# Twelve landing buffers for the expert weights, a combination of five tiles on TensorE, and separate banks for the last down product

## The chip, the cores and the metric

The kernel runs on one core of a Trainium2 chip. The metric is the device time of one execution in microseconds (us), the median of several runs. The core has TensorE (PE in the profile, its weight loads PEld), VectorE (DVE), ScalarE (ACT), GpSimd (POOL) and SyncE (SP, which issues nearly all plain DMAs), and 16 DMA engines.

## What is computed

One layer of a hybrid encoder for 1024 tokens of width 1024, in float32: a combined projection, latent attention, a spatial gating unit, an output projection, and then the part that matters here, a top-2 mixture of 32 experts, and a final RMSNorm:

```python
x = x + _hier_moe(_rmsnorm(x, g_ffn_norm[l]), ...)     # 32 experts, each token in two of them
    hid = jax.nn.silu(xb @ w_eg[e]) * (xb @ w_eu[e])   # 1024 x 256 each, for a block of 128 rows
    ys  = hid @ w_ed[e]                                # 256 x 1024
    out = zeros.at[buf_tok].add(ys * buf_w[:, None])   # the two results of a token, weighted
return _rmsnorm(x, g_final)
```

## The kernel before

The kernel is written engine by engine, in one instruction stream for each, with semaphores between them. Its stages follow one another: projection, attention, gating, output projection ("W", with the router, "R", in between), the experts ("E") and the combination ("C"). Products are made in a split float32: each operand is a high part (rounded to what TensorE multiplies in one pass) and a low part (the rest), and `mm3` (L374 to L378) issues three matmuls, high by high, low by high, high by low.

**Expert stage.** There are 36 blocks of up to 128 token rows: blocks 0 to 31 are the first of each expert, the others the overflow. `experts(eng, body)` runs the blocks on each engine in groups of four: a group written out, a loop over the middle groups, and a last group written out. A block needs three weight pieces of 1 MB (gate, up, down), so there are 108 pieces, numbered n by `piece`. A piece takes this way:

1. SP loads it into one of six landing buffers, `raw_e[n % 6]` (L499). The load waits until DVE has made the low part of piece n - 6 (`w_lo_ready`).
2. ACT writes its high part into `we_hi[n % 4]` (`high`, L1166), once TensorE has used piece n - 4 (`group_used`).
3. DVE writes its low part, landing buffer minus high part, into `we_lo[n % 4]` (`low`, L1646).
4. TensorE uses both (`columns` for gate and up, `down` for down; L376 to L378).

The token rows of a block come by an indirect DMA (a gather, L1773) from `h2_dram` into one of four buffers `xs`, three or four blocks ahead. TensorE transposes them (`rows_in`, L898), ACT and DVE split them (`rows_high` L1170, `rows_low` L1650). A block's result is copied by ACT from PSUM banks 5 and 6 to `y` (`rows_out`, L1184), and POOL sends it to `y_dram` by an indirect DMA (`scatter`, L1793), after copying a column of row numbers (`ycol`, L1789). On TensorE block j is: gate of j + 1, transposes of the hidden values of j (L918), up of j + 1, down of j, `rows_in` of j + 3. For the last two blocks the same code runs with the parts left out that have no following block.

**Combination.** For each of eight tiles of 128 tokens, SP loads the token's two expert results, `yin[t][:, 0]` and `yin[t][:, 1]` (L540), 512 KB each, behind the final gain `g_fin` (L534), once all results have been sent. DVE computes gate0 * yin0 + x2 (L1696), adds gate1 * yin1 (L1697), ACT sums the squares (L1219) and takes the root (L1221), DVE scales by it and by `g_fin` (L1706), SP stores. The fifth to eighth tile's loads wait for the first tiles' sums (`acc_ready`).

**Order around the change.** Each engine runs its stream as written; what moves work is only the order of the code and the semaphores. SP loads the first three pieces while the output projection runs, three more when its last tile is under way, and the rest in stage E.

## Time and profile before

| | us |
|---|---|
| median of 3 runs | 1217.96 (1217.54 to 1220.79) |
| the profiled execution | 1214.95 |
| its span, first to last instruction | 1213.1 |
| PE busy | 1108.3 (91% of the span) |
| DVE busy | 733.7 (60%) |
| ACT busy | 563.4 (46%) |
| POOL busy | 344.2 (28%) |

Times in the text count from the start of the span. The stages after the attention: the output projection and the router to 798, the experts from there to 1168, the combination to the end. In the experts' part PE is busy all the time and so is the DMA; in the last 43 us PE does nothing. The chain of waits (the work that ended last, followed back) is 72% PE, 12% DVE, 6% DMA and 5% ACT.

### The profile page before, as it was taken

What the parts mean: (1) busy time and instruction counts of PE and PEld (TensorE: products, weight loads), DVE (VectorE), ACT (ScalarE), POOL (GpSimd) and SP (SyncE); (2) the same over time, 40 slices, a digit from 0 to 9 for tenths busy, and PEclk for the clock granted to TensorE, in tenths of its full rate; (3) what the DMA queues carried; (4) which work ended last, traced back from release to release, by engine and by line L of the source; (5) the groups of instructions that cost most, each with busy time, mean ns of one, the idle gap of its engine ahead of it and who ended that gap; (6) DMA issues with size and microseconds to landing.
All of it is one profiled execution on the core that took longest, in us unless ns stands there. A gap on an engine that the chain in (4) does not pass through costs nothing.

```text
span 1213.1 us, 18702 instructions
## 1 busy us (share of the span) xinstructions
PE 1108.3 (91%) x6931; PEld 964.6 (80%) x6931; DVE 733.7 (60%) x948; ACT 563.4 (46%) x759; POOL 344.2 (28%) x273
## 2 busy tenths in 40 slices
PE   5998999999999999999999899979999999999930
PEld 4876888888877878888888688778999999989930
DVE  7875666666045632222112655579888888888938
ACT  6235555655135200000002322248888888778823
POOL 1403322112332222233320000034444444555310
PEclk9998999999999989999999999989999999999975
DMA  8010000020203111121102433448999999999747
GB/s 242 10 29 11 7 7 7 6 71 19 69 1 97 35 35 52 52 52 38 49 18 101 131 113 130 157 170 321 393 389 361 366 352 371 350 366 365 292 156 286
DMA packets 94174, 184.31 MB, mean 152 GB/s; under 512 B 30752, under 2 KB 68128, under 8 KB 80288
## 3 DMA queue, kind: packets, MB, share of 16 engines
q1 hardware_dynamic: 83744, 166.65, 39.2%
q0 software_dynamic: 10368, 16.80, 3.7%
q8 instruction: 42, 0.69, 0.2%
q14 instruction: 20, 0.16, 0.0%
HBM read 177.12 MB, written 27.26 MB: 168 GB/s over the span
## 4 chain that ended last, share of the span: by engine, by line
PE 72%; DVE 12%; DMA 6%; ACT 5%; issue 3%; SPq 1%; POOL 0%; ACTq 0%; DVEq 0%; POOLq 0%
PE ps L376 22%; PE ps L378 21%; PE ps L377 21%; DMA raw_e<-in_w_exp_gate_dram 4%; DVE we_lo L1646 2%; PE ps L898 2%; PE ps L666 2%; DVE pt_lo L1389 1%; PE ps L827 1%; DVE negm L1344 1%; ACT we_hi L1166 1%; DVE q_tmp L1335 1%; ACT prob L1039 1%; DVE acc L1696 1%; DVE res L1706 1%
## 5 line engine op out<-in xcount | busy, mean ns | idle before, releaser
L1646 DVE TENSOR_TENSOR we_lo<-raw_e,we_hi 128x2048 fp32r<-128x2048 f32 x108 | 246.9, 2287 | 40.2 <-ACT we_hi L1166 38.5
L1166 ACT ACTIVATE we_hi<-raw_e 128x2048 fp32r<-128x2048 f32 x108 | 206.2, 1911 | 17.7 <-DMA raw_e<-in_w_exp_gate_dram 6.7
L376 PE MATMUL ps<-ht_hi,w_hi 128*128 128x512 f32 x448 | 176.0, 393 | 0.5 <-DVE ht_lo L1262 0.4
L378 PE MATMUL ps<-ht_hi,w_lo 128*128 128x512 f32 x448 | 174.5, 389 | 0.0
L377 PE MATMUL ps<-ht_lo,w_hi 128*128 128x512 f32 x448 | 174.4, 389 | 0.0
L376 PE MATMUL ps<-we_hi,xst_hi 128*128 128x256 f32 x576 | 168.7, 293 | 0.0
L378 PE MATMUL ps<-we_hi,xst_lo 128*128 128x256 f32 x576 | 162.8, 283 | 0.0
L377 PE MATMUL ps<-we_lo,xst_hi 128*128 128x256 f32 x576 | 162.7, 283 | 0.0
L370 POOL CAST w_hi<-raw 128x1024 fp32r<-128x1024 f32 x36 | 39.5, 1097 | 297.1 <-PE ps L378 250.6
L1468 DVE TENSOR_TENSOR mix<-ps,mix 128x512 f32<-128x512 f32 x16 | 11.1, 691 | 168.1 <-PE ps L378 168.1
L376 PEld LDWEIGHTS ps<-we_hi,xst_hi 128*128 128x128 f32 x576 | 110.5, 192 | 0.2 <-issue 0.2
L377 PEld LDWEIGHTS ps<-we_lo,xst_hi 128*128 128x128 f32 x576 | 110.3, 191 | 0.0
L378 PEld LDWEIGHTS ps<-we_hi,xst_lo 128*128 128x128 f32 x576 | 110.1, 191 | 0.0
L376 PEld LDWEIGHTS ps<-ht_hi,w_hi 128*128 128x128 f32 x448 | 84.1, 188 | 18.3 <-POOL w_lo L371 0.8
L378 PEld LDWEIGHTS ps<-ht_hi,w_lo 128*128 128x128 f32 x448 | 84.1, 188 | 17.7
L377 PEld LDWEIGHTS ps<-ht_lo,w_hi 128*128 128x128 f32 x448 | 84.2, 188 | 17.2 <-issue 0.2
L371 POOL TENSOR_TENSOR w_lo<-raw,w_hi 128x1024 fp32r<-128x1024 f32 x36 | 88.3, 2454 | 2.9
L1105 ACT ACTIVATE mix<-ps 128x512 f32<-128x512 f32 x16 | 8.7, 597 | 147.0 <-PE ps L378 147.0
L1789 POOL COPY ycol<-yidx 128x1 uint32 (+1 forms) x36 | 27.4, 762 | 149.3 <-ACT y L1184 149.3
L1389 DVE TENSOR_TENSOR pt_lo<-ps,pt_hi 128x512 fp32r<-128x512 f32 (+2 forms) x96 | 50.5, 553 | 20.9 <-ACT pt_hi L1065 20.6
L376 PE MATMUL ps<-we_hi,hidt_hi 128*128 128x512 f32 x144 | 57.2, 397 | 4.8 <-DVE hidt_lo L1660 4.7
L1065 ACT ACTIVATE pt_hi<-ps 128x512 fp32r<-128x512 f32 (+2 forms) x96 | 43.5, 488 | 36.8 <-PE ps L666 36.8
(295 smaller groups left out, 2561.9 us busy)
## 6 DMA issues: line engine op xcount, KB each, us to landing
raw_e<-in_w_exp_gate_dram SPq DMA_DIRECT2D x36, 1024.0 KB
raw_e<-in_w_exp_up_dram SPq DMA_DIRECT2D x36, 1024.0 KB
raw_e<-in_w_exp_down_dram SPq DMA_DIRECT2D x36, 1024.0 KB
raw<-in_w_in_dram SPq DMA_DIRECT2D x27, 512.0 KB, 3.9
yin<-y_dram SPq DMA_DIRECT2D x16, 512.0 KB, 6.6
xin<-in_x_dram SPq DMA_DIRECT2D x8, 512.0 KB, 7.8
raw<-in_w_out_dram SPq DMA_DIRECT2D x8, 512.0 KB, 3.8
xre<-in_x_dram SPq DMA_DIRECT2D x8, 512.0 KB, 5.7
```

Of the source, the lines that this page charges most:

```text
L370: pool_link(pool, pool.tensor_copy(w_hi[n % 3][:, :, :], raw[n % 3][:, :, :]))
L371: pool.tensor_tensor(w_lo[n % 3][:, :, :], raw[n % 3][:, :, :], w_hi[n % 3][:, :, :].bitcast(F32), ALU.subtract).then_inc(sem("w_split"), 1)
L376: pe.matmul(dst, st[0], mv[0], start=first, stop=False)
L377: pe.matmul(dst, st[0], mv[1], start=False, stop=False)
L378: return pe.matmul(dst, st[1], mv[0], start=False, stop=last)
L666: mm = pe.transpose(ps[:, bank_of(0, c0 + c), (j % 4) * P:(j % 4) * P + P], prob[s % 2][:, j * P:(j + 1) * P], ident[:, :])
L898: mm = pe.transpose(ps[:, k // 4, (k % 4) * P:(k % 4) * P + P], v[:, k, :], ident[:, :])
L1065: act.activation(pt_hi[cc % 4][:, 0:w, :].rearrange("p a b -> p (a b)"), ps[:, bank_of(0, cc), 0:w * P], ACT.Copy).then_inc(sem("pt_hi_rea ...
L1166: act.activation(we_hi[c % 4][:, :], raw_e[c % 6][:, :], ACT.Copy).then_inc(sem("w_hi_ready"), 1)
L1389: dve.tensor_tensor(pt_lo[cc % 4][:, 0:w, :].rearrange("p a b -> p (a b)"), ps[:, bank_of(0, cc), 0:w * P], pt_hi[cc % 4][:, 0:w, :].rearr ...
L1646: dve.tensor_tensor(we_lo[c % 4][:, :], raw_e[c % 6][:, :], we_hi[c % 4][:, :].bitcast(F32), ALU.subtract).then_inc(sem("w_lo_ready"), 1)
L1789: pool.tensor_copy(ycol[j % 2][:, :], yidx[:, c]).then_inc(sem("ycol_ready"), 1)
```

## The change

1. **Landing buffers.** There are twelve `raw_e` (NS = 12) in place of six. `we_lo` has no buffers of its own: it lies on the landing buffer of the same piece, so DVE's subtraction writes over what it reads. The load of piece n waits for `group_used` of piece n - 12. `xs` has two buffers instead of four; the gather of block j + 4 waits for the transposes of block j + 2 instead of block j. SP issues two pieces more during the last tiles of stage W (one of them ahead of the last `xre` load, one ahead of the last store of `h2`) and four more at the start of stage E. The loop runs from 0 and adds 1 to its number.
2. **Last blocks.** On ACT and DVE the last down piece's high and low part come before SiLU and the hidden product of the last block, and ACT copies the last but one result after the last block's hidden values. The last down product goes to banks 0 and 1, and TensorE does 8 idle transposes (`keep_on`) ahead of it. POOL copies `ycol` before it waits for the result.
3. **Combination.** `g_fin` is loaded at the end of stage E. All `yin` loads are issued at once; tile 0's two halves have a semaphore each. For tiles 2, 3, 5, 6 and 7 TensorE computes gate0 * yin0 + gate1 * yin1 as four float32 matmuls with diagonal matrices `diag` (two DVE operations make them), and DVE adds `x2` from PSUM. ACT loads the table of the square root beforehand. TensorE does 64 idle transposes before these products.

```diff
+        NS = 12
+        slots = (8, 16, 24, 172, 180, 188, 196, 92, 100, 116, 124, 164)
+        raw_e = [at(f"raw_e{i}", slots[i], [P, 2048], F32) for i in range(NS)]
+        we_lo = [at(f"we_lo{i}", slots[i], [P, 2048], F32R) for i in range(NS)]
+        ON_PE = (2, 3, 5, 6, 7)
...
             for j in range(4):
                 body(0, j, lambda n: True)
             eng.wait_ge(sem("blocks_ready"), 1)
-            with eng.Fori(1, end) as it:
+            with eng.Fori(0, end) as it:
                 for j in range(4):
-                    body(it, j, lambda n: True)
+                    body(it + 1, j, lambda n: True)
...
-                    wait(sp, "w_lo_ready", n - 5)
+                    wait(sp, "group_used", n - (NS - 1))
...
                         load(0, 0, 2)
+                        load(1, 0, 2)
+                sp.wait_ge(sem("out_done"), NT + 1)
+                sp.wait_ge(sem("x2_ready"), NT + 1)
+                load(2, 0, 1)
                 sp.wait_ge(sem("h2_ready"), NT)
                 sp.dma_start(h2_dram[(NT - 1) * P:NT * P, :], ...)
...
+                sp.wait_ge(sem("group_used"), end * 12 + 1)
+                sp.dma_start(g_fin[:, :], ...)
                 for i in range(2):
                     sp.wait_ge(sem(f"y_sent{i}"), end * 32 + 32)
             if "C" in on:
-                sp.dma_start(g_fin[:, :], ...)
                 for t in range(NT):
-                    if t >= 4:
-                        sp.wait_ge(sem("acc_ready"), t - 3)
...
@@ TensorE
-                    pe.wait_ge(sem(f"xs_full{j % 4}"), (it + (j // 4 + 1)) * 16)
+                    pe.wait_ge(sem(f"xs_full{j % 2}"), (it * 2 + (j // 2 + 1)) * 16)
...
-                    wait(pe, "y_ready", it * 4 + j)
+                    wait(pe, "y_ready", it * 4 + j - last)
...
-                            mm = mm3(pe, ps[:, 5 + half, :], ...)
+                            mm = mm3(pe, ps[:, (0 if last else 5) + half, :], ...)
...
+            if "C" in on:
+                keep_on(64, 7)
+                pe.wait_ge(sem("z_diag_ready"), 3)
+                for n, t in enumerate(ON_PE):
+                    pe.wait_ge(sem(f"rows_full{t}"), 48)
+                    if n >= 2:
+                        pe.wait_ge(sem("acc_ready"), ON_PE[n - 2] + 1)
+                    for c in range(2):
+                        for k in range(2):
+                            mm = pe.matmul(ps[:, 2 * (n % 2) + c, :], diag[k][:, t, :], yin[t][:, k, c * HALF:(c + 1) * HALF],
+                                           start=k == 0, stop=k == 1)
+                    mm.then_inc(sem("spread_done"), 1)
...
@@ DVE
+                    if t in ON_PE:
+                        n = ON_PE.index(t)
+                        dve.wait_ge(sem("spread_done"), 3 + n)
+                        dve.tensor_tensor(acc[t % 2][:, :], ps[:, 2 * (n % 2):2 * (n % 2) + 2, :]..., x2[:, t, :],
+                                          ALU.add).then_inc(sem("acc_ready"), 1)
+                        return
...
@@ POOL
-                    pool.wait_ge(sem("y_ready"), it * 4 + (j + 1))
                     wait(pool, f"y_sent{j % 2}", it * 32 + 8 * (j - j % 2))
                     pool.tensor_copy(ycol[j % 2][:, :], yidx[:, c]).then_inc(sem("ycol_ready"), 1)
...
+                    pool.wait_ge(sem("y_ready"), ready)
                     pool.indirect_dma_start(y_dram, ...)
...
-                        pool.wait_ge(sem("xs_tr"), it * 4 + (j + 1))
+                        pool.wait_ge(sem("xs_tr"), it * 4 + (j + 3))
```

SP's queue from the last tiles of stage W into stage E, before (`xre` is the residual's input, `h_dram<-h` the store of a normalised tile):

```order
L508 DMA h_dram<-h_174 128x1024 [waits h2_ready]
L499 DMA raw_e_225<-in_w_exp_up_dram 128x2048 [waits mt_lo_ready]
L499 DMA raw_e_226<-in_w_exp_down_dram 128x2048
L499 DMA raw_e_227<-in_w_exp_gate_dram 128x2048
L505 DMA xre_171<-in_x_dram 128x1024 [waits x2_ready]
L508 DMA h_dram<-h_173 128x1024 [waits h2_ready]
L520 DMA h_dram<-h_174 128x1024 [waits h2_ready]
L499 DMA raw_e_222<-in_w_exp_up_dram 128x2048 [waits w_lo_ready]
L499 DMA raw_e_223<-in_w_exp_down_dram 128x2048 [waits w_lo_ready]
```

And now:

```order
L510 DMA raw_e_227<-in_w_exp_gate_dram 128x2048
L510 DMA raw_e_228<-in_w_exp_up_dram 128x2048
L516 DMA xre_171<-in_x_dram 128x1024 [waits x2_ready]
L519 DMA h_dram<-h_173 128x1024 [waits h2_ready]
L510 DMA raw_e_229<-in_w_exp_down_dram 128x2048 [waits x2_ready,out_done]
L535 DMA h_dram<-h_174 128x1024 [waits h2_ready]
L510 DMA raw_e_230<-in_w_exp_gate_dram 128x2048
L510 DMA raw_e_231<-in_w_exp_up_dram 128x2048
L510 DMA raw_e_232<-in_w_exp_down_dram 128x2048
L510 DMA raw_e_233<-in_w_exp_gate_dram 128x2048 [waits h2_stored1,h2_stored0]
L510 DMA raw_e_222<-in_w_exp_up_dram 128x2048 [waits group_used]
```

The seventh piece has moved ahead of the last `xre` load, the eighth ahead of the last store of `h2`; the ninth to twelfth follow with no wait for another engine's splitting, and from the thirteenth on a load waits for TensorE.

ACT's queue at the last two blocks, before (L1179 hidden values' high part, L1175 SiLU, L1166 a weight's high part, L1184 copy of a result):

```order
L1179 ACTIVATE hidt_hi<-ps 128x256 [waits hid_tr]
L1173 REGISTER_ALU
L1175 ACTIVATE sg<-ps 128x256 [waits hid_ready,group_used]
L1166 ACTIVATE we_hi_231<-raw_e_227 128x2048 [waits group_used,raw_e_full5]
L1182 REGISTER_ALU
L393 REGISTER_ALU [waits group_used]
L1184 ACTIVATE y_248<-ps 128x1024 [waits y_sent0]
L1179 ACTIVATE hidt_hi<-ps 128x256 [waits hid_tr]
```

And now:

```order
L1213 ACTIVATE hidt_hi<-ps 128x256 [waits hid_tr]
L1200 ACTIVATE we_hi_249<-raw_e_233 128x2048 [waits group_used,raw_e_full11]
L1207 REGISTER_ALU
L1209 ACTIVATE sg<-ps 128x256 [waits hid_ready,group_used]
L1213 ACTIVATE hidt_hi<-ps 128x256 [waits hid_tr]
L1216 REGISTER_ALU
L404 REGISTER_ALU [waits group_used]
L1219 ACTIVATE y_260<-ps 128x1024 [waits y_sent0]
```

The last weight's high part stands ahead of SiLU, and the last hidden values ahead of the copy of the last but one result.

DVE's queue for the last two tiles of the combination, before:

```order
L1696 SCALAR_TENSOR_TENSOR acc_260<-yin_257,gatew,x_172 128x1024 [waits ssq_ready,res_ready,yin_full3]
L1697 SCALAR_TENSOR_TENSOR acc_260<-yin_257,gatew,acc_260 128x1024 [waits dve_step]
L1705 RECIPROCAL rstd<-std 128x1 [waits std_ready]
L1706 SCALAR_TENSOR_TENSOR res_267<-acc_259,rstd,g_fin 128x1024 [waits dve_step]
L1705 RECIPROCAL rstd<-std 128x1 [waits std_ready]
L1706 SCALAR_TENSOR_TENSOR res_268<-acc_260,rstd,g_fin 128x1024 [waits dve_step]
```

And now:

```order
L1747 TENSOR_TENSOR acc_274<-ps,x_172 128x1024 [waits spread_done,ssq_ready,res_ready]
L1762 RECIPROCAL rstd<-std 128x1 [waits std_ready]
L1763 SCALAR_TENSOR_TENSOR res_281<-acc_273,rstd,g_fin 128x1024 [waits dve_step]
L1762 RECIPROCAL rstd<-std 128x1 [waits std_ready]
L1763 SCALAR_TENSOR_TENSOR res_282<-acc_274,rstd,g_fin 128x1024 [waits dve_step]
```

One addition from PSUM, which waits for TensorE, stands in the place of two operations on the loaded rows; so it is for the five tiles named.

## Rows read from the trace of the kernel before

**Rows 1.** Busy time of each engine in stretches of the span, in us.

```profile
core 0: us, PE busy (x) PEld busy (x) DVE busy (x) ACT busy (x) POOL busy (x), PEclk, DMA share, GB/s
775.00:798.00 23.00, 15.35 (x91) 12.54 (x90) 13.44 (x50) 8.71 (x11) 0.00 (x0) 0.90 0.12 47
...
839.00:1022.00 183.00, 183.00 (x1332) 173.57 (x1332) 162.83 (x117) 154.26 (x133) 82.72 (x76) 1.00 0.99 374
1022.00:1094.00 72.00, 69.64 (x501) 65.23 (x501) 60.38 (x43) 57.59 (x50) 34.92 (x28) 1.00 0.97 359
...
1170.00:1213.00 43.00, 0.00 (x0) 0.00 (x0) 31.50 (x32) 12.72 (x25) 0.00 (x0) 0.50 0.80 305
```

**Rows 2.** The same view for L898 alone: PE, PEld, clock, DMA share, GB/s.

```profile
839.20:1142.90 303.70, 33.25 (x256) 33.01 (x256) 1.00 0.98 372
```

**Rows 3.** Chain of waits: start, us, what; L898 x8 transposes one block's rows.

```profile
839.45 0.88 PE ps L898 x8
...
868.31 0.88 PE ps L898 x8
...
1027.67 16.02 DMA raw_e<-in_w_exp_gate_dram
...
1141.94 0.88 PE ps L898 x8
```

**Rows 4.** Timeline of ACT: start, us, line, what, idle before and its releaser.

```profile
1033.35 1.92 ACT L1166 ACTIVATE we_hi<-raw_e 128x2048 fp32r<-128x2048 f32 x1 [0.43 <-DMA raw_e<-in_w_exp_gate_dram]
```

**Rows 5.** Timeline of DVE, SP and POOL at the start of the experts.

```profile
782.34 0.69 DVE L1505 TENSOR_TENSOR x<-ps,xre 128x512 f32<-128x512 f32 x1
...
792.07 0.33 SPq L520 DMA_DIRECT2D h_dram<-h  x1
...
799.45 2.55 POOL L1773 DMA_INDIRECT xs<-h_dram,xidx  x1 [33.57 <-DVE xidx L1594]
```

**Rows 6.** The last `xre` load, issued at 765.2: issue to landing.

```profile
DMA to landing us min/median/max: 10.6/10.6/10.6
```

**Rows 7.** Timeline of POOL: a gather within the expert stage.

```profile
855.06 1.04 POOL L1773 DMA_INDIRECT xs<-h_dram,xcol  x1 [0.76 <-POOL xcol L1778]
```

**Rows 8.** Timeline of ACT and of PE at the last block.

```profile
1157.86 1.91 ACT L1166 ACTIVATE we_hi<-raw_e 128x2048 fp32r<-128x2048 f32 x1
1161.34 0.38 ACT L1179 ACTIVATE hidt_hi<-ps 128x256 fp32r<-128x256 f32 x1
...
1162.67 0.47 PE L376 MATMUL ps<-we_hi,hidt_hi 128*128 128x512 f32 x1 [2.14 <-DVE hidt_lo L1660]
```

**Rows 9.** Timeline of POOL, last scatter; then the chain's next DMA.

```profile
1167.81 0.98 POOL L1793 DMA_INDIRECT y_dram<-y,ycol  x1 [0.76 <-POOL ycol L1789]
...
1170.83 6.05 DMA yin<-y_dram
```

**Rows 10.** The load of `g_fin`, issued at 1170.0: issue to landing.

```profile
DMA to landing us min/median/max: 4.3/4.3/4.3
```

**Rows 11.** DMA in the combination; columns as in group 1.

```profile
1180.00:1185.00 5.00, 0.00 (x0) 0.00 (x0) 4.53 (x5) 3.68 (x7) 0.00 (x0) 0.50 1.03 413
```

**Rows 12.** Last step of the chain; DVE's last operation; additions from PSUM in W.

```profile
1207.06 1.16 ACT junk L1219 x2
...
1208.77 1.28 DVE L1706 SCALAR_TENSOR_TENSOR res<-acc,rstd,g_fin 128x1024 f32<-128x1024 f32 x1
...
L1505 DVE TENSOR_TENSOR x<-ps,xre x9: 691/1225/1225, 686.3 to 788.3; 128x1024 f32<-128x1024 f32 x7, 128x512 f32<-128x512 f32 x2
```

**Rows 13.** Timeline of PE: two float32 matmuls (four records) at full clock.

```profile
63.35 1.88 PE L590 MATMUL ps<-z_diag,ones 128*128 128x512 f32 x4
```

**Rows 14.** PE after a pause; then the clock, as in group 1.

```profile
426.99 0.77 PE L376 MATMUL ps<-ot_hi,w_hi 128*128 128x512 f32 x1 [4.24 <-issue]
...
428.00:431.00 3.00, 3.00 (x9) 2.33 (x8) 0.69 (x1) 0.27 (x1) 0.00 (x0) 0.50 0.00 0
432.00:435.00 3.00, 3.00 (x15) 2.47 (x14) 0.10 (x1) 0.00 (x0) 0.00 (x0) 1.00 0.00 0
```

More of the change, by code:

```diff
@@ L522, in expert @@
                 def expert(it, j, left):
-                    if left(2):
+                    fetched = isinstance(it, int) and it == 0 and j == 0
+                    if left(2) and not fetched:
                         load(1, it, j + 2)
-                    if left(1):
+                    if left(1) and not fetched:
                         load(2, it, j + 1, not left(2))
+                    if isinstance(it, int) and it == 0 and j == 1:
+                        for i in range(2):
+                            sp.wait_ge(sem(f"h2_stored{i}"), 16 * NT // 2)
                     if left(3):
@@ L1183, in rows_out @@
                     wait(act, f"y_sent{j % 2}", it * 32 + 8 * (j - j % 2))
-                    act.activation(y[j % 2][:, :], ps[:, 5:7, :].rearrange("p b c -> p (b c)"), ACT.Copy).then_inc(sem("y_ready"), 1)
+                    b = 0 if last else 5
+                    act.activation(y[j % 2][:, :], ps[:, b:b + 2, :].rearrange("p b c -> p (b c)"), ACT.Copy).then_inc(sem("y_ready"), 1)
                 def expert(it, j, left):
@@ L1189, in expert @@
                         high(1, it, j + 2)
-                    if left(1):
+                    if left(2):
                         silu(it, j + 1)
-                        high(2, it, j + 1, not left(2))
+                        high(2, it, j + 1)
+                    elif left(1):
+                        high(2, it, j + 1, True)
+                        silu(it, j + 1)
+                        return
+                    else:
+                        rows_out(it, j - 1, False)
                     rows_out(it, j, not left(1))
```

95 lines of the change are left out of this document (57 added, 38 removed).

## Prediction

> **What bounds the kernel now.** I first read the busy time by stretch, to see which engine sets the pace where. From 839 to 1022 us TensorE is busy in every one of the 183 us, at full clock, and the DMA share is 0.99; from 1022 to 1094 TensorE is idle for 2.4 us of 72 and the DMA share is still 0.97 [rows 1]. So two things run side by side: TensorE, and a DMA that has hardly a free moment. Then the chain of waits shows the rhythm. The transposes of a block's rows begin at 839.45, and those three blocks on at 868.31: one block in 9.62 us [rows 3]. Up to 1142 there are 256 of them, 32 blocks of 8, so 31 intervals [rows 2]; they end with the block at 1141.94 [rows 3]. At 9.62 us they would take 298.2 us; they took 1141.94 - 839.45 = 302.5. The stage loses 4.3 us against its own rhythm. Where: after 1022 the chain goes through a weight load that took 16.02 us from issue to landing [rows 3], and from 1033 on ACT waits for a landing before each split [rows 4]; before that, in the 183 us at 100% TensorE, nothing was lost. So the landing buffers run empty late in the stage, and the rest of the stage is TensorE's own. Last, the stretch from 1170 on: 43 us with TensorE at zero, DVE busy 31.5 us and the DMA at 0.80 [rows 1]. There DVE is the bound, after some 7 us of waiting for the first load.
>
> The sums are made against the profiled execution: span 1213.1, time 1214.95. The median of the runs, 1217.96, is 3.0 us above it, and I take the difference over to the median unchanged. About 0.3% (3.7 us) is what a measurement of this kernel can tell from no change.
>
> **Twelve landing buffers.** A load of piece n could run ahead of ACT's split by five pieces (six buffers, freed by DVE); now by eight (twelve buffers, freed by TensorE, and ACT's split waits for piece n - 4). Three pieces are one block, 9.62 us more of slack. The shortfall to cover is 4.3 us. The lead has to be built while the DMA is free, for in the stage it is not: between 775 and 798 its share is 0.12 [rows 1], and a 1 MB piece takes 2.5 us at the 413 GB/s of [rows 11]. The two pieces moved into stage W and the four issued at its end are 15 us of transfer, which fit mostly ahead of 806. So I take the whole 4.3 us as gained: **-4.3 us** (bounds: 0, if the DMA is short throughout the stage, and -4.3, since the rhythm of 9.62 us is TensorE's). The first loads in the loop wait for TensorE instead of DVE; SP has nothing else queued behind them in this stage. DVE's subtraction in place has the same size, so the same price.
>
> What the moved loads are in the way of: the last `xre` load was issued at 765.2 and landed 10.6 us later [rows 6], behind three pieces; a fourth makes it 778.3, and DVE reads it at 782.34 [rows 5]: 4 us of cover. The last store of `h2`, issued at 792.07, gets a piece ahead of it, 2.5 us at most; POOL did not wait for it but for DVE's row numbers, until 799.45 [rows 5]: hidden, by about 2 us. The first gather, at 799.45, shares the DMA with the end of pieces nine to twelve, where it shared it with pieces seven and eight before; I take **0**, between -1 us (the warming transposes of TensorE end about then) and +2.5 us (one piece in its way). The loop's other bounds leave TensorE's register instructions in number as they were.
>
> `xs` with two buffers: a gather now waits for the transposes of block j + 2. These run just ahead of the moment at which POOL comes to the gather anyway (in the block before 868.31's but one, transposes at 849.07 = 868.31 - 2 x 9.62, the gather at 855.06 [rows 3, 7]), so it costs 0.
>
> **The last block.** Today ACT splits the last down weight at 1157.86, behind SiLU, copies the last but one result, and comes to the last hidden values at 1161.34; TensorE starts the last down product at 1162.67, after 2.14 us idle [rows 8]. In the new order the hidden values' high part follows their transposes, which end when TensorE goes idle at 1160.5, without the copy between, and the weight is split before: ACT starts it at 1160.5 or a little after instead of 1161.34, and TensorE about 0.9 us earlier. The eight idle transposes (an eighth of a rows' transposing each, 0.88 / 8 us [rows 3]) take 0.9 us, within that pause. **-0.9 us** (0 to -1.2). For the last scatter the column of row numbers is copied beforehand, and the 0.76 us of waiting for it [rows 9] leaves the path: **-0.8 us**.
>
> **Start of the combination.** When the last scatter has landed, SP issues `g_fin` (1170.0) and the first tile, and DVE starts when a load issued at 1170.83 has landed 6.05 us later, at 1176.9 [rows 9]. `g_fin` alone took 4.3 us [rows 10]: that is the time of 512 KB on an empty queue. In the new order the first half of tile 0 stands first on an empty queue, and DVE's first operation needs it alone. With 1.7 us gained above, SP issues it at 1168.3, it lands at 1172.6, and DVE starts 4.3 us earlier than now: **-2.6 us** beyond the 1.7.
>
> **The combination.** For five tiles two DVE operations of 1.28 us give way to one addition from PSUM, which took 1.23 us in stage W [rows 12]; DVE alone would save 5 x 1.3 = 6.6 us. But TensorE and the loads may now be later, so I write out the schedule, on the old time scale (without the 4.3 us). A tile is 1.05 MB, 2.55 us at 413 GB/s [rows 11]; tiles are complete at 1173.9, 1176.4, 1179.0, 1181.5, 1184.1, 1186.6, 1189.1, 1191.7. A float32 matmul of 512 columns is two records; four records took 1.88 us with the last one's tail, 0.43 each from start to start [rows 13]. A tile has four matmuls, eight records: 3.4 us at full clock, 6.8 at half. The 64 idle transposes keep TensorE at work to about 1172, then it waits for tile 2 until 1179.0; after a pause of 4.24 us it stood at 1.2 GHz, and came back to 2.4 GHz within 5 us of work [rows 14]. I take 3.5 us at half clock: tile 2 takes 5.2 us, to 1184.2; then 3.4 each: tile 3 to 1187.6, tile 5 to 1191.0, tile 6 to 1194.4. Tile 7 needs the PSUM banks of tile 5, so DVE's sum of it.
> DVE: tile 0 to 1175.3, tile 1 (from 1176.5) to 1179.1, scaling of 0 to 1180.5. It waits for TensorE, adds tile 2 at 1184.2, scales 1, to 1186.9; tile 3 and scaling 2 from 1187.6 to 1190.3; tile 4 (its own, two operations) and scaling 3 some 4.1 us, to 1194.4; then a pair of 1.23 and 1.28 and the reciprocal, 2.8 us: 5 and 4 to 1197.2, 6 and 5 to 1200.0. Tile 7 on TensorE from 1195.7 to 1199.1: ready. It is summed at 1201.3; the square and the root take 1.7 us (from 1207.06, when the sum was there, to 1208.77 [rows 12]), and the last scaling ends at 1204.3. Before, it ended at 1208.77 + 1.28 = 1210.05 [rows 12]. Of these 5.8 us, 4.3 are the earlier start; the combination itself gives **-1.5 us** (-3 with TensorE at full clock throughout). The two operations that make `diag` (1.2 us each, by the same kind of addition) lie under the last down product and the last scatter, where DVE is idle. The final stores: 4.2 MB, 10 us of transfer from 1191.7 on, done before DVE's last one.
>
> **Sum:** -4.3 - 0.9 - 0.8 - 2.6 - 1.5 = -10.1 us. The profiled execution would take 1204.9, the median 1217.96 - 10.1 = 1207.9.
>
> **Rivals.** *The DMA is short throughout, so the larger buffers only move the wait* (or are never ahead, since loads wait for TensorE): then 4.3 us come back, 1212.2. For it speaks the share of 0.99 even before 1022; against it that the shortfall of 4.3 us is smaller than the four pieces, 10 us, that now land before the stage needs them.
> *TensorE stays at 1.2 GHz in the combination.* Five tiles in a row of 6.8 us from 1179.0 end at 1213.0; plus the addition, 1.7 and the scaling, 1217.2 instead of 1210.05: with the gain of the experts 1217.96 + 7.2 - 4.3 = 1220.9. Against it: [rows 14], where steady work brought the clock back in under 5 us.
> *Gathers come too late* (slower). Place: `rows_in`, on TensorE. The gather at 855.06 is for the transposes at 868.31 [rows 3, 7], 13.2 us later. If a deeper queue of weights holds a gather up, each microsecond beyond 13.2 is lost in each of some 28 blocks. If it had to let eight pieces of 3.2 us pass, 25.7 us, the stage would take 28 x 12.5 = 350 us more; at 14 us of latency 22 us more, about 1234. Decisive is whether the gather waits behind the weights. A weight piece took 16.02 us at 1027 [rows 3] and TensorE never stood still for rows in that stretch, so gathers were faster than the weights queued ahead of them: it is unlikely. The Trainium skill ("DMA: Bandwidth & Descriptors", Queues, rings and completion order) says that an engine takes turns between the rows of queues that have work; by that rule a longer queue of weights doesn't delay a gather, and the trace agrees, as the 16.02 us beside the 13.2 show.
> *Better:* TensorE at full clock from tile 2 on, and the first gather a little earlier: 1204 to 1205.
>
> **Chances.** The forecast (1205 to 1210.5) 0.68; better 0.08; the DMA short, or the start of the experts delayed by a piece (1210.5 to 1213) 0.14; TensorE at half clock (1220.9, within 0.3% or just above) 0.05; gathers late 0.05. So faster by over 0.3% (below 1214.3) 0.90, within 0.3% 0.05, slower 0.05. Range 1203.5 to 1212.5: it leaves out the last two and the edge of the third.
>
> **What would show it.** Right: 31 intervals of 9.62 us for L898's successor, without a DMA in the chain and without ACT waiting for weights after 1000; the last down product 1.2 us after TensorE's last transposes of hidden values instead of 2.1; DVE's first combining operation 4.4 us after the first tile's issue; DVE waiting for TensorE before tiles 2 and 3 by some 4 and 1 us, and not after. Wrong: ACT still waiting for landings late in the stage (first rival); PEclk at 0.5 to the end (second); PE idle before the rows' transposes, released by the gather (third).

## The result, and the profile after

The changed kernel takes **1206.24 us** (median of 4 runs, 1205.61 to 1207.88); the kernel before, over all its runs by then, 1217.75. The ratio is 0.9908, with a 95% interval of 0.9891 to 0.9926. The forecast was 1207.9, the range 1203.5 to 1212.5. The profiled execution took 1206.01, its span is 1204.1, so the two profiled executions lie 8.9 us apart and the medians 11.5.

The busy time by stretch, columns as in [rows 1], which these lines answer to; then the same for L917 alone (L898 before, [rows 2]):

```profile
core 0: us, PE busy (x) PEld busy (x) DVE busy (x) ACT busy (x) POOL busy (x), PEclk, DMA share, GB/s
775.00:798.00 23.00, 15.35 (x93) 12.53 (x91) 13.47 (x50) 8.71 (x11) 0.00 (x0) 0.90 0.48 178
839.00:1022.00 183.00, 183.00 (x1333) 173.58 (x1332) 162.86 (x115) 154.14 (x134) 117.71 (x76) 1.00 0.98 370
1022.00:1094.00 72.00, 72.00 (x526) 68.29 (x525) 63.07 (x46) 60.92 (x53) 45.93 (x31) 1.00 0.99 379
...
1172.00:1179.00 7.00, 3.10 (x4) 1.51 (x5) 3.92 (x4) 2.82 (x6) 0.00 (x0) 0.52 1.02 416
1179.00:1200.00 21.00, 16.16 (x37) 6.57 (x35) 17.28 (x21) 8.66 (x18) 0.00 (x0) 0.99 0.80 317
```

```profile
840.30:1139.80 299.50, 33.25 (x256) 33.14 (x256) 1.00 0.96 365
```

TensorE now works through all of 1022 to 1094, where it stood idle for 2.4 us, and the DMA moves 379 GB/s there in place of 359. Ahead of the stage, from 775 to 798, the DMA share is 0.48 in place of 0.12. In the last stretch TensorE is at work, but from 1172 to 1179 at 1.2 GHz.

The chain of waits (start, us, what), beside [rows 3]:

```profile
799.61 8.68 DMA xs<-h_dram,xidx
808.33 1.17 PE ps L917 x8
...
840.69 0.88 PE ps L917 x8
...
1138.90 0.88 PE ps L917 x8
...
1161.65 1.03 ACT y L1219
1162.75 0.49 issue
1163.46 2.08 DMA y_dram<-y,ycol
...
1175.90 8.74 PE ps L990 x16
1184.76 1.22 DVE acc L1747
```

From 840.69 to 1138.90 are 298.21 us, which is 31 times 9.62 within 0.01 us; no weight load is in the chain any more. New in it are the first gather, 8.68 us, and TensorE's products of the combination.

The last block on ACT and on PE, and the last scatter on POOL, beside [rows 8] and [rows 9] (timeline: start, us, line, what, idle before and its releaser):

```profile
1157.53 0.38 ACT L1213 ACTIVATE hidt_hi<-ps 128x256 fp32r<-128x256 f32 x1 [2.60 <-PE ps L937]
...
1158.62 0.47 PE L382 MATMUL ps<-we_hi,hidt_hi 128*128 128x512 f32 x1 [0.25 <-DVE hidt_lo L1702]
...
1163.46 0.98 POOL L1854 DMA_INDIRECT y_dram<-y,ycol  x1 [1.77 <-ACT y L1219]
```

And the combination on DVE and PE, beside [rows 12]:

```profile
1169.30 1.28 DVE L1751 SCALAR_TENSOR_TENSOR acc<-yin,gatew,x 128x1024 f32<-128x1024 f32 x1 [8.66 <-DMA yin<-y_dram]
1173.23 1.28 DVE L1751 SCALAR_TENSOR_TENSOR acc<-yin,gatew,x 128x1024 f32<-128x1024 f32 x1 [1.32 <-DMA yin<-y_dram]
1181.33 1.22 DVE L1747 TENSOR_TENSOR acc<-ps,x 128x1024 f32<-128x1024 f32 x1 [4.11 <-PE ps L990]
1184.76 1.22 DVE L1747 TENSOR_TENSOR acc<-ps,x 128x1024 f32<-128x1024 f32 x1 [0.82 <-PE ps L990]
...
1175.90 15.59 PE L990 MATMUL ps<-yin,diag 128*128 128x512 f32 x32 [7.30 <-DMA yin<-y_dram]
1192.82 3.67 PE L990 MATMUL ps<-yin,diag 128*128 128x512 f32 x8 [1.33 <-DVE acc L1747]
```

DVE waits for TensorE before tiles 2 and 3, by 4.11 and 0.82 us, and never after: the waits that the prediction named.

By its own steps the difference of the spans is:

| step | forecast | measured | from |
|---|---|---|---|
| start of the experts | 0 | +1.2 | first rows' transposes 807.08, now 808.33 |
| landing buffers | -4.3 | -4.3 | 302.5 us less 298.2 |
| last block | -0.9 | -1.0 | last rows' transposes to last down product, 20.9, now 19.9 |
| last scatter | -0.8 | -0.3 | end of the copy of `y` to the scatter, 1.11, now 0.79 |
| start of the combination | -2.6 | -3.3 | last scatter to DVE's first operation, 9.17, now 5.84 |
| combination | -1.5 | -1.4 | DVE's first operation to its end, 33.07, now 31.70 |
| sum | -10.1 | -9.1 | |

The sizes agree. Whether the reasons do is another matter, and the experiments are about that.

### The profile page after: what moved, and what is told of

Its sections match the earlier page's. It is cut to its first block, busy times and chain, and to the rows that moved or that the text cites. A ratio compares the mean times of both kernels' runs of the same rounds, so it can differ in the third digit from the quotient of the medians.

```text
span 1204.1 us, 18947 instructions
## 1 busy us (share of the span) xinstructions
PE 1133.5 (94%) x7043; PEld 979.9 (81%) x7043; DVE 727.3 (60%) x945; ACT 563.0 (47%) x760; POOL 391.5 (33%) x271
## 4 chain that ended last, share of the span: by engine, by line
PE 79%; DVE 10%; ACT 5%; issue 3%; DMA 2%; SPq 1%; POOL 0%; ACTq 0%; POOLq 0%; DVEq 0%
PE ps L382 23%; PE ps L384 23%; PE ps L383 23%; PE ps L917 3%; PE ps L685 2%; DVE pt_lo L1431 1%; PE ps L846 1%; DVE negm L1386 1%; DVE q_tmp L1377 1%; ACT prob L1072 1%; PE ps L990 1%; DMA xs<-h_dram,xidx 1%; DVE we_lo L1688 1%; PE ps L694 1%; PE ps L937 1%
## 5 line engine op out<-in xcount | busy, mean ns | idle before, releaser
L376 POOL CAST w_hi<-raw 128x1024 fp32r<-128x1024 f32 x36 | 39.3, 1091 | 297.4 <-PE ps L384 250.5
L384 PEld LDWEIGHTS ps<-ht_hi,w_lo 128*128 128x128 f32 x448 | 84.1, 188 | 17.6
L1854 POOL DMA_INDIRECT y_dram<-y,ycol x36 | 39.4, 1096 | 112.8 <-ACT y L1219 106.6
L1835 POOL COPY xcol<-xidx 128x1 uint32 (+1 forms) x32 | 71.8, 2242 | 3.2 <-PE ps L917 2.6
L1431 DVE TENSOR_TENSOR pt_lo<-ps,pt_hi 128x512 fp32r<-128x512 f32 (+2 forms) x96 | 50.5, 553 | 20.9 <-ACT pt_hi L1098 20.7
L1846 POOL COPY ycol<-yidx 128x1 uint32 (+1 forms) x36 | 61.3, 1704 | 0.0
```

The costliest lines, as they stand in the source:

```text
L376: pool_link(pool, pool.tensor_copy(w_hi[n % 3][:, :, :], raw[n % 3][:, :, :]))
L384: return pe.matmul(dst, st[1], mv[0], start=False, stop=last)
L1431: dve.tensor_tensor(pt_lo[cc % 4][:, 0:w, :].rearrange("p a b -> p (a b)"), ps[:, bank_of(0, cc), 0:w * P], pt_hi[cc % 4][:, 0:w, :].rearr ...
L1835: pool.tensor_copy(xcol[j % 4][:, :], xidx[:, c]).then_inc(sem("xcol_ready"), 1)
L1846: pool.tensor_copy(ycol[j % 2][:, :], yidx[:, c]).then_inc(sem("ycol_ready"), 1)
L1854: pool.indirect_dma_start(y_dram, bass.IndirectOffsetOnAxis(ycol[j % 2][:, :], 0), y[j % 2][:, :], None, bounds_check=last_row, oob_is_err ...
```

## The experiments

The stages ahead of the experts vary by up to 5.5 us between executions, so the parts of the span are compared, not the spans. Seven of the kernels below, named in brackets where each is described, ran once, profiled: hold_loads took 1208.78 us, warm 1210.29, no_pe 1209.93 and ycol_late 1209.90, beside 1220.14 for the kernel before; late_build 1208.75, dve_free 1212.53 and before_again 1219.68, beside 1217.71 (median of 11 runs of the kernel before). One execution each doesn't rank them; what they show is read from their traces.

**Do the four early pieces delay the first gather?** (hold_loads) Pieces nine to twelve wait for it:

```diff
             if "E" in on:
+                sp.wait_ge(sem("xs_full0"), 16)
```

> The changed kernel, but SP waits until the first gather of rows has landed before it issues the ninth to twelfth weight piece. In the changed kernel that gather took 8.68 us from issue to landing (799.61 to 808.3) and the first transposes of rows began at 808.33, 1.25 us later than before the change. Theory (the four pieces that now stand in the queue at 793 to 808 share the DMA with the gather): the gather lands within 5 to 6 us, the first transposes begin at 806.3 to 807, where the idle transposes ahead of them end, and the span is 1.2 to 2 us shorter than 1204.1, with no wait for weights later. Rival (the gather's time is that of making its descriptors on POOL, beside DVE): 808.3 and 1204.1 as they are.

The first gather lands 5.56 us after its issue, where it took 8.68 in the changed kernel and 7.6 before. From its issue to the rows' transposes are 6.60 us in place of 8.72. PE's timeline shows what is last now:

```profile
801.17 8.44 PE L969 MATMUL ps<-ident 128*128 128x128 f32 x64
809.45 1.04 PE L919 MATMUL ps<-ident,xs 128*128 128x128 f32 x8
```

The rows' transposes follow the idle ones without a gap: the gather is off the path, and the 64 idle transposes, the first 2.6 us of them at half clock, are on it. 2.1 us are gained, and nothing is lost against the rhythm later. The theory holds: the loss in the first line of the table is the new pieces' work. The size differs from trace to trace: from the gather's issue to the rows' transposes are 7.9 to 10.3 us in the eight traces of changed kernels with all twelve pieces issued ahead (10.3 in no_pe), 7.3 to 7.6 in the kernel before (two traces) and in late_build, and 6.6 to 7.5 in the three with the four pieces held.

**Does the clock set the price of TensorE's products?** (warm) More idle transposes, so that no pause is left ahead of them:

```diff
-                keep_on(64, 7)
+                keep_on(128, 7)
```

> The changed kernel with 128 idle transposes instead of 64 before the five tiles' products, so that TensorE works up to about 1176, when tile 2 lands. Theory (TensorE fell to 1.2 GHz at 1172.3, 3.7 us after the transposes ended, and the first 3.3 us of products ran at that clock): the clock stays at 2.4 GHz, the first two tiles' products take 6.9 us instead of 8.74, DVE's waits of 4.11 and 0.82 us shrink by 1.6 us in all, and the span is 1.3 to 1.9 us shorter. Rival 1 (transposes don't hold the clock up): as it is. Rival 2 (DVE's order is the bound behind these waits): the waits shrink, the end stays.

```profile
1172.00:1180.00 8.00, 7.72 (x71) 7.48 (x69) 4.27 (x4) 1.45 (x3) 0.00 (x0) 1.00 0.98 365
1180.00:1200.00 20.00, 17.91 (x40) 7.35 (x40) 16.35 (x19) 8.43 (x18) 0.00 (x0) 1.00 0.95 383
...
1180.93 7.11 PE L990 MATMUL ps<-yin,diag 128*128 128x512 f32 x16 [1.21 <-DMA yin<-y_dram]
...
1178.26 1.28 DVE L1751 SCALAR_TENSOR_TENSOR acc<-yin,gatew,x 128x1024 f32<-128x1024 f32 x1 [2.21 <-DMA yin<-y_dram]
1184.74 1.22 DVE L1747 TENSOR_TENSOR acc<-ps,x 128x1024 f32<-128x1024 f32 x1 [2.48 <-PE ps L990]
```

The clock column stays at 1.00 (the idle transposes end 1.2 us before the first product), two tiles' products take 7.11 us in place of 8.74, and DVE waits 2.48 us before tile 2 in place of 4.11. The theory on the clock and the waits holds. The end didn't follow by as much: DVE's first operation to its last takes 30.95 us in place of 31.70, 0.75 less and not 1.3 to 1.9. The loads of tiles 1 and 2 landed 0.9 us later in this trace (DVE waited 2.21 us for tile 1's, and 1.32 in the changed kernel's trace), and that took the rest back.

**What is TensorE's part worth?** (no_pe) All eight tiles on DVE, as before; the rest of the change stays:

```diff
-        ON_PE = (2, 3, 5, 6, 7)
+        ON_PE = ()
```

> The changed kernel with all eight tiles combined on DVE, as before the change; the loads stay as changed (all issued at once, the gain first, two semaphores for tile 0). It measures the combination on TensorE by itself. Theory (from the first operation to the last DVE needed 33.07 us before and 31.71 with TensorE, and the loads are not the bound): 32.7 to 33.1 us, 1.0 to 1.4 us longer than the changed kernel, span 1205.1 to 1205.5. Rival (the five tiles save DVE 6.6 us of work, and what is lost are waits that would be there anyway, since the loads were the bound): 36 us or more.

DVE's first operation comes 5.9 us after the last scatter, as in the changed kernel, but the second tile's comes only at 1175.04, after 2.00 us for its load:

```profile
1170.43 1.28 DVE L1751 SCALAR_TENSOR_TENSOR acc<-yin,gatew,x 128x1024 f32<-128x1024 f32 x1 [8.68 <-DMA yin<-y_dram]
1175.04 1.28 DVE L1751 SCALAR_TENSOR_TENSOR acc<-yin,gatew,x 128x1024 f32<-128x1024 f32 x1 [2.00 <-DMA yin<-y_dram]
```

From the last scatter's start to the last result are 40.3 us, where the kernel before took 42.2. So of the 3.3 us by which DVE starts earlier, 1.9 arrive at the end and the rest turns into this wait. Both expectations missed: from the first operation to the last DVE needed 34.4 us, not up to 33.1 and not 36, since the loads were the bound for one tile. The changed kernel's 31.70 are 2.7 us less, so TensorE's part is worth about twice the 1.4 of the table above. The products on TensorE give what lies between 40.3 and each of the last column. The second column is how long TensorE's granted clock stood at 1.2 GHz after its pause; the third is the time from the last scatter's start to the first product, which waits for tile 2's loads; the fourth that of tile 2's products, from their start to tile 3's:

| kernel | half clock, us | scatter to first product, us | tile 2's products, us | scatter to end, us |
|---|---|---|---|---|
| before, and once more | no products on PE | | | 42.2, 42.5 |
| no_pe | no products on PE | | | 40.3 |
| hold_loads, ycol_late, lead9, lead7, late_build | 10.2 | 13.5, 13.7, 13.4, 14.1, 12.9 | 5.9, 5.8, 6.5, 5.1, 5.8 | 39.3, 39.4, 39.9, 39.2, 38.6 |
| changed, changed once more, dve_free | 6.8 | 12.4, 12.6, 12.9 | 5.1, 5.4, 5.2 | 37.5, 37.9, 38.1 |
| warm, both | none | 13.3, 12.8 | 3.5, 3.5 | 36.8, 36.3 |

TensorE's part gives 0.5 to 1.7 us in the first group, 2.3 to 2.8 in the second, 3.5 to 4.0 in the third. The length of the dip is only a part of that. The third and fourth columns add up, with 20.0 us that are the same in all ten traces, to the last: what counts is when tile 2 has landed, and how much of the half clock lies under its products. lead7 shows it, with a dip of 10.2 us; its last scatter starts at 1164.33:

```profile
1178.43 15.60 PE L990 MATMUL ps<-yin,diag 128*128 128x512 f32 x32 [8.96 <-DMA yin<-y_dram]
```

Its products took as long as the changed kernel's (15.59 us), since they too met only the last 3.3 us of the dip; its 1.7 us more come from the first product's start alone, 14.1 us after the scatter in place of 12.4.

**The last scatter.** (ycol_late) POOL waits for the result first and copies `ycol` behind that, as before:

```diff
+                    pool.wait_ge(sem("y_ready"), it * 4 + (j + 1))
...
                     pool.tensor_copy(ycol[j % 2][:, :], yidx[:, c])...
-                    pool.wait_ge(sem("y_ready"), ready)
```

> The changed kernel with POOL's old order in the scatter: wait for the result first, then copy the column of row numbers. I had forecast 0.8 us for the last scatter; the traces show 1.11 us from the end of the result's copy to the scatter's start before and 0.79 after. Theory (most of the 0.76 us of waiting for the column was POOL's own time ahead of any indirect DMA, which stays): 1.1 us again, span 0.3 us longer. Rival (the new order brought 0.8, and something else took 0.5 away): 0.8 us longer. In the loop the gathers come later by up to 2.4 us; neither theory expects TensorE to wait for rows.

```profile
1164.51 0.19 POOL L1847 COPY ycol<-yidx 128x1 uint32 x1 [1.35 <-ACT y L1219]
1165.45 0.98 POOL L1851 DMA_INDIRECT y_dram<-y,ycol  x1 [0.76 <-POOL ycol L1847]
```

The scatter starts 1.10 us after the copy of `y` has ended, as before (1.11), and 0.79 in the changed kernel. The order gives 0.3 us. The 0.76 us that the profile shows as a wait for `ycol` are mostly POOL's own time ahead of an indirect DMA: without the copy the chain still has 0.49 us of "issue" there.

**The changed kernel once more** (after_again), on the chip of the three that follow.

> The changed kernel once more, as the measure for the three beside it on the same chip. Expected: 31 intervals of 9.62 us in the expert stage, 8.7 us from the first gather's issue to the first transposes, 31.7 us of combination with a dip of TensorE's clock that lasts 7 to 10 us (6.9 us in the changed kernel's first trace, 10.2 us in two kernels of the last job).

Median 1208.47 of 10 runs (1202.24 to 1211.12), ratio 0.9918 (0.9895 to 0.994): as the first time. No loss against the rhythm, 8.25 us from the gather's issue to the transposes, a dip of 6.8 us.

**How much lead do the loads need?** With the pieces ahead of the stage left as they are, a load is issued five pieces (lead9) or three (lead7) before ACT's split, in place of eight:

```diff
-                    wait(sp, "group_used", n - (NS - 1))
+                    wait(sp, "group_used", n - ((NS - 1) if isinstance(n, int) and n < 12 else 8))
```

(lead7 has 6 in place of 8.)

> Twelve landing buffers, the same loads ahead of the stage, but from piece 12 on a load waits until TensorE has used piece n - 9 in place of n - 12: it is issued some five pieces (16.0 us) before ACT splits it, as in the kernel before, in place of eight (25.6 us). In the changed kernel the weights' latency from issue to landing grew from 9 to 14.95 us through the stage. My theory (the buffers only need to cover the latency, which comes to just 16 us at the end): no stall or up to 1 us over the stage, so 0 to 1 us above the changed kernel. Rival A (the lead of eight pieces is what gained the 4.3 us): the stage loses 4 us again against its rhythm of 9.62 us, as before. Rival B (the gain came from the four to six pieces loaded before the stage, which leave less to be carried in it): no difference at all.

> As the one before, but from piece 12 on a load waits until TensorE has used piece n - 7: it is issued some three pieces (9.6 us) before ACT splits it. My theory: the latency of 9 to 15 us is longer than that from about piece 22 on, so ACT waits for landings from 860 us on and the stage goes at the pace of the DMA, which in the changed kernel landed a piece each 3.24 us in place of the 3.207 us that TensorE takes: 3 to 8 us of stall over the stage, the smaller the more the latency falls with the shorter queue. Rival (the lead decides nothing, what was loaded ahead decides): less than 1 us of stall.

lead9: median 1208.68, ratio 0.9922 (0.9896 to 0.9948), and 31 intervals of 9.62 us: nothing lost. ACT never waited for a landing. So the lead of the kernel before is enough, and eight pieces are not needed: my first theory held, rival A fell, and rival B still stood. lead7: median 1210.93, ratio 0.9943 (0.9921 to 0.9965). Its profiled execution lost 0.5 us, not the 3 to 8 expected, and within its rival's 1 us; ACT's waits there, in us, times and longest, against none in lead9:

```profile
ACT we_hi L1200 <- DMA raw_e<-in_w_exp_gate_dram: 3.4, 6, 0.8
ACT we_hi L1200 <- DMA raw_e<-in_w_exp_down_dram: 2.5, 5, 0.7
ACT we_hi L1200 <- DMA raw_e<-in_w_exp_up_dram: 1.9, 5, 0.5
```

But that left a riddle: the kernel before had lead9's lead and lost 4.3 us. Either the pieces loaded ahead make the difference, or who releases the loads. Two kernels tell these apart.

**Without the early pieces** (late_build: twelve buffers, TensorE releases, six pieces ahead):

```diff
-                    wait(sp, "group_used", n - (NS - 1))
+                    if isinstance(n, int) and 6 <= n < 12:
+                        sp.wait_ge(sem("w_lo_ready"), n - 5)
+                    else:
+                        wait(sp, "group_used", n - (NS - 1))
...
-                        load(1, 0, 2)
-                sp.wait_ge(sem("out_done"), NT + 1)
-                sp.wait_ge(sem("x2_ready"), NT + 1)
-                load(2, 0, 1)
...
             if "E" in on:
+                load(1, 0, 2)
+                load(2, 0, 1)
```

> The changed kernel with only six pieces loaded ahead of the expert stage: pieces 6 to 11 wait for DVE's low part of piece n - 6, as in the kernel before, and from piece 12 on TensorE's use of piece n - 12 lets a load go, so that the lead of twelve buffers can only be built within the stage. What the prediction said (the DMA has no free moment in the stage, so the lead has to be built ahead of it): a piece lies about 6 us in its buffer before ACT splits it at the start of the stage (6.3 us at piece 18 in the kernel before, 17.6 in the changed one), it falls to zero by about piece 75, and 2 to 4 us are lost against the rhythm of 9.62 us. Rival (the DMA can carry more than it was asked for, the six buffers only didn't let it): the time in the buffer grows to 10 us or more within the first blocks, and nothing is lost.

**With the old release** (dve_free: twelve buffers, twelve pieces ahead, DVE's low part releases):

```diff
-                    wait(sp, "group_used", n - (NS - 1))
+                    if isinstance(n, int) and n < 12:
+                        wait(sp, "group_used", n - (NS - 1))
+                    else:
+                        sp.wait_ge(sem("w_lo_ready"), n - 5)
```

> The changed kernel's loads ahead of the stage, but from piece 12 on a load waits for DVE's low part of piece n - 6, as in the kernel before. It differs from the kernel lead9 (released by TensorE's use of piece n - 9, nothing lost, 8.6 us in the buffer at piece 18 and 4.4 at the least) only in who lets the load go. My theory: as long as nobody waits for a landing, the two releases come at about the same time, DVE's some 2 us later, since it splits as late as ACT does: 6 to 8 us in the buffer at piece 18, 1 to 4 us at the least, and 0 to 1 us lost; what was loaded ahead makes no difference after the first blocks, since the lead is cut to the same length again. Rival (the early loads bring the gain): 12 us or more in the buffer at piece 18.

**And the kernel before once more** (before_again):

> The kernel before once more, for a second trace on the chip of these experiments, where its runs lie between 1209.7 and 1222.3 us. Expected: the loss against the rhythm of 9.62 us differs from the 4.3 us of the first trace, by up to 3 us either way, since a piece took between 3.22 and 3.32 us to land in the kernels so far; the rest (last block, last scatter, combination of 42.2 us from the last scatter) as before within 0.5 us. If it is larger here, that explains why the medians of the two kernels lie 11.5 us apart and their first traces 9.

The "time in the buffer" is from a piece's landing to the start of ACT's split of it:

| kernel | released by | buffer at piece 18 / 60 / 96, us | lost in the stage, us |
|---|---|---|---|
| before | DVE, n - 6 | 6.3 / 2.0 / 0.1 | 4.3 |
| before_again | DVE, n - 6 | 6.5 / 2.2 / 0.1 | 4.9 |
| dve_free | DVE, n - 6 | 5.4 / 0.6 / 0.1 | 5.0 |
| lead9 | TensorE, n - 9 | 8.6 / 8.4 / 5.5 | 0 |
| lead7 | TensorE, n - 7 | 1.0 / 2.1 / 0.1 | 0.5 |
| late_build | TensorE, n - 12 | 8.7 / 9.9 / 7.1 | 0 |
| changed | TensorE, n - 12 | 17.6 / 16.8 / 11.4 | 0 |

The same in the view of a stretch of dve_free and of lead9, and in ACT's waits of dve_free (us, times, longest):

```profile
1000.00:1130.00 130.00, 127.28 (x913) 119.26 (x913) 110.47 (x79) 105.07 (x91) 66.95 (x53) 1.00 0.96 362
...
1000.00:1130.00 130.00, 130.00 (x949) 123.39 (x948) 115.38 (x82) 109.61 (x97) 85.62 (x56) 1.00 0.99 380
```

```profile
ACT we_hi L1203 <- DMA raw_e<-in_w_exp_gate_dram: 9.5, 12, 1.0
ACT we_hi L1203 <- DMA raw_e<-in_w_exp_down_dram: 9.2, 11, 1.2
ACT we_hi L1203 <- DMA raw_e<-in_w_exp_up_dram: 3.2, 10, 0.6
```

dve_free has all twelve buffers and all the early pieces and loses 5.0 us, as much as the kernel before. late_build has none of the early pieces and loses nothing. All three executions with DVE's release lost 4.3 to 5.0 us, all eleven with TensorE's (the experiments and both of the changed kernel) 0 to 0.5. So it is the release that brings the 4.3 us. My expectations missed in both: I gave late_build 2 to 4 us of loss (its rival was right in that, though the time in the buffer didn't grow to 10 us early) and dve_free at most 1.

A part of the mechanism can be read. ACT goes through its queue in order, so one that waits for a landing has the hidden values queued behind it, and TensorE waits for those; the row is from before_again:

```profile
PE ps L376 <- DVE hidt_lo L1660: 3.1, 6, 0.6
```

With DVE's release the same wait also holds up the next loads, since DVE's low part follows ACT's high part. That closes a loop of six buffers. For pieces 74 to 97 it takes, in the kernel before, 15.7 us from issue to landing, 0.1 in the buffer, 1.9 for ACT and 2.3 for DVE: 20.0, or 3.34 us a piece, where TensorE takes 3.21; the landings lie 3.36 us apart (3.40 in before_again, 3.35 in dve_free). In lead7 ACT waits too, 7.8 us in all, but loads are issued on TensorE's beat and it costs 0.5. **What stays open** is why the buffers run empty at all: already between pieces 24 and 60, with nobody waiting, the time in the buffer falls by 2.9 to 4.2 us with DVE's release, and changes by -0.5 to +2.5 with TensorE's. On TensorE's 3.207 us a piece that makes landings 3.29 to 3.32 us apart against 3.14 to 3.22, for the same bytes. With DVE's release the loads are issued some 1.4 to 2 us later against the gathers and scatters (dve_free against lead9); whether this is the cause was not tried.

before_again brought another thing. TensorE's last down product took 4.6 us in it, and 3.0 in the first trace:

```profile
1165.53 0.47 PE L376 MATMUL ps<-we_hi,hidt_hi 128*128 128x512 f32 x1 [2.14 <-DVE hidt_lo L1660]
...
1167.40 0.63 PE L376 MATMUL ps<-we_hi,hidt_hi 128*128 128x512 f32 x1
...
1166.60:1169.80 3.20, 3.20 (x9) 2.26 (x7) 0.00 (x0) 0.00 (x0) 0.14 (x1) 0.50 0.03 4
```

After the idle 2.14 us the clock fell to 1.2 GHz for 3.4 us, in the middle of the product. With 0.25 us idle and the eight idle transposes ahead, none of the twelve traces of the changed kernel and its variants shows it. So where the clock falls, the change is worth 1.6 us more. That and the 0.6 us of greater loss in the stage make up nearly all by which the second pair of traces lies further apart than the first: spans of 1217.9 and 1206.6, 11.3 us, as the medians of the first comparison.

**The two small edits together** (both): the held loads and 128 idle transposes.

> Pieces nine to twelve are issued once the first gather has landed, and TensorE does 128 idle transposes ahead of the combination's products in place of 64. The parts have been run one at a time: the first shortened the way from the first gather's issue to the first transposes from 8.7 to 6.6 us, the second kept TensorE's clock at full and made the combination 30.95 us long in place of 31.7 (33.4 with the longer dip of the clock). My theory: the two lie one behind the other on the path and add up: 2.1 us and 0.75 to 2.4 us, so 2.9 to 4.5 us below the changed kernel on the same chip, at a median of about 1203. Rival: the weights that come later are missed in the expert stage, whose DMA has little to spare: then ACT waits for landings after 1000 us and the 2.1 us are lost again, which leaves 0.8 to 2.4 us.

Median 1206.94 of 6 runs, ratio 0.9901 (0.9869 to 0.9934), 1.5 us below the changed kernel beside it, less than the 2.9 expected. In the traces it is 0.9 us from the gather's issue to the transposes (7.34 us for 8.25: the half clock lasted 10.2 us there, and the idle transposes 9.2) and 1.6 in the combination (36.3 for 37.9). No wait came back in the stage.

**Another choice of tiles** (best). Tiles 3, 4, 6 and 7 on TensorE, with the two edits and 152 idle transposes (the edit against the kernel before this one):

```diff
-        ON_PE = (2, 3, 5, 6, 7)
+        ON_PE = (3, 4, 6, 7)
...
-                keep_on(128, 7)
+                keep_on(152, 7)
```

> The held loads and the longer run of idle transposes (152 in place of 128), and tiles 3, 4, 6 and 7 on TensorE in place of 2, 3, 5, 6 and 7. In the kernel with both small edits DVE waited 2.48 us for TensorE before tile 2 and 0.82 us before tile 3, since tile 2 lands only at 1177.7 and its products take 3.55 us; DVE's own two operations on it would have ended as early. My theory: tile 2 by DVE costs 1.35 us more of DVE's time and takes away the 3.3 us, tile 4 on TensorE in place of tile 5 costs nothing, and some 0.7 us of waiting before tile 3 and 0.9 us before tile 4 stays. From the last scatter to the last result 36.3 - 3.3 + 1.35 + 0.7 = 35.0 to 35.9 us, where it was 36.3; the whole about 0.4 to 1.3 us below the kernel with both edits (1206.9). Rival: TensorE falls to half clock while it waits for tile 3, some 1 us after its idle transposes end; then its products take 7 us and DVE waits 3 us more: 38 to 39 us.

```profile
1184.88 1.23 DVE L1749 TENSOR_TENSOR acc<-ps,x 128x1024 f32<-128x1024 f32 x1 [1.01 <-PE ps L992]
1188.32 1.23 DVE L1749 TENSOR_TENSOR acc<-ps,x 128x1024 f32<-128x1024 f32 x1 [0.82 <-PE ps L992]
```

Median 1204.47 of 6 runs, ratio 0.9884 (0.9865 to 0.9904), the lowest of all, though its interval overlaps with the others'. The choice of tiles has no part in it that the trace would show: scatter to end is 36.4 us, as with five tiles (36.3), and the 35.0 to 35.9 expected were not reached. DVE's waits for TensorE fell from 3.30 to 1.83 us, 1.47 less, and its own two operations on tile 2 cost 1.35 more. I had taken 0.7 for the wait of 1.01, and had added the rest up too low.

## Why the prediction was right

Landing buffers, last block and combination came out within 0.1 us, the three other terms 1.2, 0.5 and 0.7 us off; the sum was 1.0 us too large against the two profiled executions, and 1.4 us too small against the medians, which lie 11.5 us apart. The terms' errors partly cancel: 1.2 and 0.5 us one way, 0.7 the other.

- **Landing buffers:** the size was right and half of the reason wrong. The loss to cover was read rightly from the chain and from ACT's waits, and the rhythm of TensorE was its bound. But "three pieces are one block, 9.62 us more of slack" is not what covers it (lead9 has none of it and loses nothing), and "the lead has to be built while the DMA is free" fell with late_build. The step that did it stands in the prediction in half a sentence, as a matter of no weight: the loads "wait for TensorE instead of DVE"; the first rival even takes it for a danger ("or are never ahead, since loads wait for TensorE"). The first rival (the DMA short throughout) is out too: at 380 GB/s it kept up in lead9, with 362 in dve_free. The number of buffers is not without weight: TensorE's release with the old six would leave a lead of two pieces, which was not run, and with three (lead7) ACT already waits.
- **Start of the experts:** 0 was chosen between -1 and +2.5, and it was +1.2. What failed was the choice of the middle: the row that would have priced it was [rows 6], where a small load behind three pieces took 10.6 us. Holding the four pieces gives 2.1 us back in hold_loads and 0.9 in the run called both, where TensorE's idle transposes ahead ran longer at half clock.
- **Last block:** right to 0.1 us. Not foreseen was that the shorter pause keeps the clock up, 1.6 us in executions like before_again.
- **Last scatter:** mis-sized, 0.3 us for 0.8. The wait in [rows 9] was taken for the copy's whole price.
- **Start of the combination:** -3.3 for -2.6, as the first half tile landed in 3.6 us, not 4.3. Why it was faster than `g_fin` is open; behind both the next load follows 0.4 us later. Of that only 1.9 would reach the end without TensorE's part, since the second tile's load is late.
- **Combination:** -1.4 for -1.5. The products began at 1175.90 and ran 3.3 us at half clock (forecast 3.5), two tiles took 8.74 us (forecast 5.2 + 3.4), and DVE waited 4.11 and 0.82 us (forecast 4 and 1). But that it came to -1.4 was luck. The five traces with the dip of 10.2 us, where tile 2 also landed 0.4 to 1.7 us later, would give -0.3 to +1.0 for this term. And it is no measure of TensorE's part, which is worth 2.8 us here: 1.4 of them only make good what the earlier start loses again to loads that come later.
- **Gathers too late,** the slower rival: no. Beside weights that took 11 to 14 us late in the stage, a gather took 8.4 us (lead9) and 8.5 (changed), against the 13.2 it has; in late_build, where weights took 16 to 20 us, it was 8.3 at the median. By the Trainium skill ("DMA: Bandwidth & Descriptors", Queues, rings and completion order) a DMA engine takes turns between the queues that have work; the traces agree in that gathers pass the weights, but the first gather's 5.6 us alone and 8.7 us beside four pieces show that a turn is not free.

## What to carry to other kernels

When loads fall behind, ask first who releases the buffer, and only then how many there are: a release by the engine that sets the pace keeps the loads on its beat, while one behind an engine that itself waits for landings closes a loop that makes each late load delay the next. That the release decides is shown for this kernel; why its buffers ran down before anybody waited is not. A change of the order of loads ahead of a stage should be held against the first small, urgent transfer that follows, which here took 3 us longer beside four pieces that nobody needed yet. And work put on an idle engine comes at the clock that this engine has after its pause: keep it busy up to its first operand, and put it on the tiles whose operands land early enough.

## What the runs showed of the hardware

- TensorE's granted clock fell to 1.2 GHz for 3.4, 6.8 or 10.2 us at a time. After the pause in the combination it was 6.8 us in both traces of the changed kernel and in dve_free, and 10.2 in five variants with the same 64 idle transposes. A pause of 2.14 us was followed by a dip of 3.4 us in one execution of two.
- Idle transposes kept the clock at 2.4 GHz: the column stands at 1.00 from 1172 to 1180 in warm, where hardly anything else ran.
- POOL's copy of one column of row numbers took 0.19 us at the end of ycol_late, with DVE idle. Within the expert stage it mostly took 0.4 to 1.7 us in the kernel before and 1.9 to 2.3 in the changed one, where the copies start at other moments of DVE's work. That DVE is the cause was not tried; TensorE never waited for it.
